# Four pairs of PSUM banks for the up products, and the last output slice finished by column halves

## The reference

```python
up = rms_norm(x, g_ffn_norm) @ w_up              # (512 + 32) x 1024 times 1024 x 5632
up_c, ffn_buf_new = causal_dwconv(up, ffn_buf, ffn_conv_w, ffn_conv_b)   # width 3
gate, val = jnp.split(up_c, 2, axis=-1)
x = x + (jax.nn.silu(gate) * val) @ w_down       # times 2816 x 1024
```

## Time and profile before

| | us |
|---|---|
| three runs, median (lowest to highest) | 945.11 (944.52 to 946.34) |
| the profiled execution, its own time | 945.21 |
| its span, first to last instruction | 943.3 |
| PE busy in it | 899.4 |
| up products, about | 527 to 799 |
| down products, about | 800 to 938 |

### The profile page before, as it was taken

How to read it: one execution, slowest core, us unless ns; L and a number is a source line. 1 busy time by engine, 2 the same in 40 slices (tenths; PEclk the granted TensorE clock), 3 DMA queues, 4 the chain that set the end, 5 groups by cost and what they waited for, 6 DMA issues and landing times.

```text
span 943.3 us, 18508 instructions
## 1 busy us (share of the span) xinstructions
PE 899.4 (95%) x6689; PEld 847.8 (90%) x6689; DVE 604.8 (64%) x1182; ACT 347.5 (37%) x619; POOL 238.3 (25%) x278
## 2 busy tenths in 40 slices
PE   5999999998799999998999999999999999999998
PEld 5899999987577887776799999999999999999998
DVE  4378634686789888897544488777778777322221
ACT  6331455364344444442423533333333332112111
POOL 4000233462333221331012233333333333201000
PEclk8999999999899999997999999999999999999999
DMA  8333323322000000010003232233332222233321
GB/s 256 79 84 76 97 78 82 77 73 46 15 7 10 14 14 14 20 27 1 1 23 90 67 110 78 81 88 89 89 89 82 78 85 84 84 97 104 98 70 36
DMA packets 114630, 63.55 MB, mean 67 GB/s; under 512 B 7836, under 2 KB 113054, under 8 KB 114588
## 3 DMA queue, kind: packets, MB, share of 16 engines
q1 hardware_dynamic: 112396, 59.17, 22.4%
q0 software_dynamic: 2192, 3.81, 1.8%
HBM read 59.85 MB, written 2.70 MB: 66 GB/s over the span
## 4 chain that ended last, share of the span: by engine, by line
PE 86%; DVE 6%; issue 4%; ACT 2%; POOL 1%; SPq 1%; DMA 0%; DVEq 0%; ACTq 0%; POOLq 0%
PE PS L1141 61%; PE PS L1354 4%; PE PS L1338 4%; PE PS L1319 3%; PE PS L1176 3%; PE PS L1265 2%; PE PS L1308 2%; PE PS L1214 2%; PE PS L1261 1%; PE PS L1362 1%; PE PS L1292 1%; PE PS L1283 1%; DVE small L1010 1%; DVE w_lo L773 0%; PE PS L1325 0%
## 5 line engine op out<-in xcount | busy, mean ns | idle before, releaser
L541 ACT ACTIVATE w_hi<-w_raw 128x1024 fp32r<-128x1024 f32 (+2 forms) x104 | 107.6, 1035 | 368.7 <-PE PS L1141 354.4
L773 DVE TENSOR_TENSOR w_lo<-w_raw,w_hi 128x1024 fp32r<-128x1024 f32 (+2 forms) x104 | 128.1, 1231 | 122.8 <-ACT w_hi L541 122.6
L1141 PE MATMUL PS<-x2h,w_hi 128*128 128x274 f32 x704 | 147.7, 291 | 1.1 <-DVE w_lo L773 1.1
L1141 PE MATMUL PS<-x2h,w_lo 128*128 128x274 f32 x704 | 146.9, 290 | 0.0
L1141 PE MATMUL PS<-x2l,w_hi 128*128 128x274 f32 x704 | 146.9, 290 | 0.0
L1141 PEld LDWEIGHTS PS<-x2h,w_hi 128*128 128x128 f32 x704 | 111.9, 189 | 1.4 <-issue 1.3
L1141 PEld LDWEIGHTS PS<-x2l,w_hi 128*128 128x128 f32 x704 | 112.0, 189 | 0.0
L1141 PEld LDWEIGHTS PS<-x2h,w_lo 128*128 128x128 f32 x704 | 111.4, 189 | 0.0
L1141 PE MATMUL PS<-xnh,w_hi 128*128 128x274 f32 x384 | 83.3, 299 | 4.4 <-DVE w_lo L773 2.3
L1141 PE MATMUL PS<-xnl,w_hi 128*128 128x274 f32 x384 | 81.7, 295 | 0.0
L1141 PE MATMUL PS<-xnh,w_lo 128*128 128x274 f32 x384 | 81.0, 293 | 0.0
(11 more groups left out here) (254 smaller groups left out, 1706.6 us busy)
## 6 DMA issues: line engine op xcount, KB each, us to landing
w_raw<-in_w_up_dram SPq DMA_DIRECT2D x44, 512.0 KB, 3.8
w_raw<-in_w_in_dram SPq DMA_DIRECT2D x24, 512.0 KB, 3.9
w_raw<-in_w_down_dram SPq DMA_DIRECT2D x16, 512.0 KB, 3.7
w_raw<-in_w_out_dram SPq DMA_DIRECT2D x8, 512.0 KB, 4.1
w_raw<-in_w_down_dram SPq DMA_DIRECT2D x8, 384.0 KB, 3.9
xnat<-in_x_prompt_dram SPq DMA_DIRECT2D x4, 512.0 KB, 5.0
w_raw<-in_w_in_dram SPq DMA_DIRECT2D x4, 416.0 KB, 4.7
wq<-in_w_q_b_dram SPq DMA_DIRECT2D x8, 192.0 KB, 2.5
```

Of the source, the lines that this page charges most:

```text
L541: nc.scalar.activation(hi[:, slot % 2, 0:n], raw[:, slot % 4, 0:n], ACT.Copy).then_inc(s_hi, 1)
L773: tt(lo[:, slot % 2, 0:n], raw[:, slot % 4, 0:n], hi[:, slot % 2, 0:n].bitcast(F32), ALU.subtract).then_inc(s_lo, 1)
L1141: last = mm(PS[:, 2 * rank + j, 0:HT], w[:, slot % 2, cols], x[:, k0 + k, j * HT:(j + 1) * HT], start=(k0 + k == 0 and first), stop=(k0 + ...
```

## The change

Two parts. **Up:** product r uses banks 2r and 2r+1 for r = 0 to 3 (`up_pair`), PE waits for the evacuation of the product four before it, and waits in addition on `s_ms` before the first use of banks 4 and 5 and on `s_stc` before that of banks 6 and 7. **Tail:** product 7 is written out as `last_product`. Its first two items run as before; the transposes of slice 6 are moved behind the first item; the 36 matmuls of the last item run as 18 for the left column half and then 18 for the right. DVE adds the residual by halves, PE transposes frames 0 to 255 and then frames 256 to 511 with the sample's (`last_y`, banks 6, 0 and 1), ACT copies the two parts, SP stores each part. The sample's rows are copied by DVE and stored by the POOL queue.

```diff
+        def up_pair(r):
+
+            return PS[:, 2 * r:2 * r + 2, 0:HT]
...
-            for m in range(KD - 2, KD):
-                sp.wait_ge(s_yn, 2 * m + 2)
-                sp.dma_start(y_p[:, :, m * P:(m + 1) * P], ynat[:, m % 2, 0:NT, :]).then_inc(s_ylast, 16)
-                sp.dma_start(o[1][0][:, m * P:(m + 1) * P], ynat[0:DEC, m % 2, NT, :]).then_inc(s_ylast, 16)
+            m = KD - 2
+            sp.wait_ge(s_yn, 2 * m + 2)
+            sp.dma_start(y_p[:, :, m * P:(m + 1) * P], ynat[:, m % 2, 0:NT, :]).then_inc(s_ylast, 16)
+            sp.dma_start(o[1][0][:, m * P:(m + 1) * P], ynat[0:DEC, m % 2, NT, :]).then_inc(s_ylast, 16)
+            m = KD - 1
+            for part in range(2):
+                sp.wait_ge(s_yn, 2 * m + 1 + part)
+                sp.dma_start(y_p[:, 2 * part:2 * part + 2, m * P:(m + 1) * P], ynat[:, m % 2, 2 * part:2 * part + 2, :]).then_inc(s_ylast, 16)
             sp.wait_ge(s_ylast, 16 * 4)
...
-            pool.wait_ge(s_out, 16 * 6)
+            m = KD - 1
+            pool.wait_ge(s_ysample, 1)
+            pool.dma_start(o[1][0][:, m * P:(m + 1) * P], ynat[0:DEC, m % 2, NT, :]).then_inc(s_out, 16)
+            pool.wait_ge(s_out, 16 * 7)
...
-            y_natural(KD - 1, (KD - 1) % 2)
+            last, s = KD - 1, (KD - 1) % 2
+            act.wait_ge(s_yout[s], 32 * (last // 2))
+            for part in range(2):
+                act.wait_ge(s_yt, last + 1 + part)
+                nc.scalar.activation(ynat[:, s, 2 * part:2 * part + 2, :], PS[:, (6, 0)[part], 0:2 * P].rearrange("p (a b) -> p a b", a=2), ACT.Copy).then_inc(s_yn, 1)
...
-                    tt(halves(u_r[:, LEAD:]), pair(r), halves(rsT[:, :]), ALU.mult).then_inc(s_free, 1)
+                    tt(halves(u_r[:, LEAD:]), up_pair(r), halves(rsT[:, :]), ALU.mult).then_inc(s_free, 1)
...
-                dve.wait_ge(s_used, I_DOWN + 3 * (m + 1))
                 if m >= 2:
                     dve.wait_ge(s_yt, m - 1)
+                if m == KD - 1:
+                    for j in range(2):
+                        dve.wait_ge(s_used, I_DOWN + 3 * (m + 1) + j)
+                        cols = slice(j * HT, (j + 1) * HT)
+                        tt(yT[:, m % 2, cols], PS[:, 2 * (m % 2) + j, 0:HT], xT[:, m, cols], ALU.add).then_inc(s_free, 1)
+                    break
+                dve.wait_ge(s_used, I_DOWN + 3 * (m + 1))
                 tt(halves(yT[:, m % 2, :]), pair(m), halves(xT[:, m, :]), ALU.add).then_inc(s_free, 1)
+
+            last, s = KD - 1, (KD - 1) % 2
+            dve.wait_ge(s_yt, last + 2)
+            dve.wait_ge(s_yout[s], 32 * (last // 2))
+            nc.vector.tensor_copy(ynat[0:DEC, s, NT, :], PS[0:DEC, 1, 0:P]).then_inc(s_ysample, 1)
...
             for r in range(4):
-                pe.wait_ge(s_free, G_UP + r - 1)
-                product(x2h, x2l, r % 2, [(I_UP + r, r, 0, KD)], (s_xl, KD) if r == 0 else None, x2_sums if r == 0 else None)
+                pe.wait_ge(s_free, G_UP + min(r - 1, 0))
+                if r == 2:
+                    pe.wait_ge(s_ms, 1)
+                if r == 3:
+                    pe.wait_ge(s_stc, 1)
+                product(x2h, x2l, r, [(I_UP + r, r, 0, KD)], (s_xl, KD) if r == 0 else None, x2_sums if r == 0 else None)
             with pe.Fori(1, NU // 4) as it:
-                products(it, G_UP, x2h, x2l)
+                for r in range(4):
+                    pe.wait_ge(s_free, it * 4 + (G_UP + r - 3))
+                    product(x2h, x2l, r, [(it * 4 + (I_UP + r), r, 0, KD)])
...
+            def last_product(m):
+
+                x_parts = ((hi, hh), (hi, hl), (lo, hh))
+                for j, q in ((None, 0), (None, 1), (0, 2), (1, 2)):
+                    k0, slot = KD * q, (3 * m + q) % 2
+                    pe.wait_ge(s_lo, I_DOWN + 3 * m + q + 1)
+                    for k in range(k0, min(k0 + KD, KF)):
+                        cols = slice((k - k0) * P, (k - k0 + 1) * P)
+                        for n, (w, x) in enumerate(x_parts):
+                            for jj in (0, 1) if j is None else (j,):
+                                last = mm(PS[:, 2 * (m % 2) + jj, 0:HT], w[:, slot, cols], x[:, k, jj * HT:(jj + 1) * HT],
+                                          start=(k == 0 and n == 0), stop=(k == KF - 1 and n == 2))
+                    last.then_inc(s_used, 1)
+                    if q == 0:
+                        y_transpose(m - 1)
+
+            def last_y(m):
+
+                s = m % 2
+                pe.wait_ge(s_yn, 2 * m - 2)
+                for part in range(2):
+                    pe.wait_ge(s_free, G_DOWN + m + 1 + part)
+                    for t, (c0, _, n) in list(enumerate(TOK))[2 * part:2 + 3 * part]:
+                        dst = PS[0:n, (6, 0)[part], t % 2 * P:(t % 2 + 1) * P] if t < NT else PS[0:n, 1, 0:P]
+                        last = nc.tensor.transpose(dst, yT[:, s, c0:c0 + n], ident[:, :])
+                    last.then_inc(s_yt, 1)
+
             for m in range(KD):
                 items = [(I_DOWN + 3 * m + q, 3 * m + q, KD * q, min(KD, KF - KD * q)) for q in range(3)]
-                pe.wait_ge(s_free, G_DOWN + m - 1)
+                pe.wait_ge(s_free, G_DOWN + (m - 3 if m < 2 else m - 1))
+                if m == KD - 1:
+                    last_product(m)
+                    last_y(m)
+                    break
...
-            y_transpose(KD - 1)
```

More of the change, by code:

```diff
@@ L272, in layer @@
         s_gc, s_sg, s_h2, s_hh, s_hl = sem("gate_conv"), sem("gate_silu"), sem("hidden"), sem("hidden_hi"), sem("hidden_lo")
-        s_yt, s_yn = sem("y_transposed"), sem("y_natural")
+        s_yt, s_yn, s_ysample = sem("y_transposed"), sem("y_natural"), sem("last_sample_natural")
         block = ctx.enter_context(nc.Block())
```

## The result

The changed kernel took 950.37 us (median of 6 runs, 948.85 to 951.0) against 944.82 us for the kernel before beside it: a ratio of 1.0057, interval 1.0043 to 1.0071. It is slower by 0.6%, and 4 us above the range that was given.

The account below looks back on a forecast made before the run. TensorE, busy 899.4 of 943.3 us, was taken to bound the kernel. Up 0; tail +0.55, -0.30, -0.22, -0.38 and the stores' landing came to about -0.4 us: median 944.7 us, range 943.5 to 946.1.

Parts of the forecast that it names:

- The up part: Up products through four pairs of banks: worth 0, since TensorE's only wait there names w_lo, not a bank.
- the gap: TensorE's wait before the third up product, 1.07 us, for w_lo; claimed to stay.
- The bound of 0.3 us for short pauses: Up products: most that pauses too short for the wait list could cost over 2148 matmuls, from the pitch difference.
- Steps 1 to 7 of the tail: Last product to SP's stores: transposes uncovered +0.55 us, half add -0.30, fewer transposes -0.22, shorter copy -0.38; landing at 942.17.
- Step 8: Sample's last rows: VectorE copies, POOL issues the store at 940.17, landing 2.2 us later at 942.37, the last landing.
- Rival 2: POOL's sample store lands last after 4.0 us: +1.3 us, 946.4 us; chance 0.09.
- rival 3: The 36 last-item matmuls into one bank don't overlap, pitch 0.29 us: +5.8 us, 950.5 us; chance 0.02.
- Step 9: End of span: 0.42 us after the last landing gives 942.79; POOL noticing up to 0.27 us later, half counted: 942.9.
- three signs of being wrong: Gap at 540 us closes, the 36 matmuls take over 4.7 us, or POOL's store takes more than 2.7 us.

Follow-up runs that it names:

- e3: Kernel before with only the up products' rotation through four pairs of banks; 945.54 us, ratio 0.9994.
- e7: Kernel before (two pairs of banks) with VectorE making the w_lo split before the evacuation in an up product; 945.25 us, ratio 1.0006.
- e8: Changed kernel with the sample's last store on SP, plus VectorE's w_lo split put before the evacuation (four pairs); 943.97 us, ratio 0.9989.
- e1: Changed kernel with the sample's last store issued by the SP queue behind its two parts instead of by POOL; 944.11 us, ratio 0.9986.
- e5: The changed kernel measured again, nothing altered; 949.35 us, ratio 1.0046 to the kernel before.
- e2: Kernel before with one more wait at the end of POOL's list, no transfer added or moved; 946.62 us, ratio 1.0014.
- e6: Changed kernel with POOL still issuing the sample's store but SP waiting for its landing; 947.39 us, ratio 1.0026.

## Why the prediction was wrong

**The up part** was right in all: no row had TensorE waiting for a bank, the gap named w_lo and stayed, and e3 measured no change. The bound of 0.3 us for short pauses wasn't needed: with four pairs the 2148 matmuls took 274.68 us (e3), with two 274.69. e7 and e8 confirm the reading of the gap from the other side.

**Steps 1 to 7 of the tail** were right in sign and nearly in size. From the mark to the last matmul the changed kernel took 0.56 us more (405.89 against 405.33), for the five transposes whose cover was gone. The 36 matmuls into one bank cost nothing. In the changed kernel they start from 935.44 us on:

```profile
935.57 0.29 PE L1483 MATMUL PS<-hl,w_hi 128*128 128x274 f32 x1
...
939.79 0.29 PE L1483 MATMUL PS<-hl,w_hi 128*128 128x274 f32 x1
```

Between these two are 33 steps, 4.22 us, 127.9 ns each. The right add took 0.44, three transposes 0.55, the copy 0.38 us (0.36 expected). The stores landed sooner than assumed, 128 KB in 1.8 us and not 2.2. With the sample on SP (e1) all this comes to -0.8 us from the mark, where the forecast said -0.4 and -0.8 at best.

**Step 8** had POOL's issue right (941.90 against 940.17 + 1.7 for the later start) and its landing too long (1.9 us, not 2.2). Rival 2, which feared the landing, did not come true. Nor did rival 3, although its time of 950.5 us is nearly the measured 950.37: that is chance, since its mechanism, a longer pitch in one bank, was absent.

**Step 9 is the one that failed.** "With the 0.42 us of the end: 942.79. POOL may notice the landing up to 0.27 us later than SP did (0.30 against 0.03)." The 0.42 us was read from an execution in which SP was the last to finish, and was given to one in which POOL is. In its place came 0.2 us until POOL's list was over, its DRAIN of 4.72 us, and 0.3 us to the end of the span: 5.2 us in place of 0.4 to 0.7. In step 8 the text says of POOL's queue that "all that is queued behind is its own wait for landings"; behind that wait stood the DRAIN, which no line of the code names. The row was there in the trace of the kernel before, at L112, 4637 ns long and hidden under product 7: its cover, 12.9 us between its end and the span's, was the thing to ask for when POOL's list was made to last to the end. With it, and with nothing but the rows of the kernel before, the sum reads 942.37 + 0.42 + 4.64 = 947.4 us, 4.2 us over the span of 943.3, and a forecast of 949.3 us. None of the three signs of being wrong that the prediction named appeared: the gap stayed, the 36 matmuls took 4.6 us and POOL's store 1.9. Signs can only be named for terms that the sum has, and the DRAIN was not one of them.

The medians gave 4.6 and 5.5 us where the profiles give 4.0. The second interval (3.1 to 5.7) holds 4.0, the first (4.1 to 6.7) just misses it. That the rest is scatter of the start is what e5 and the spread of the marks suggest; it is not shown run by run.

**The range.** It was said to join the forecast's bounds with the scatter of the runs. These give 944.3 - 0.6 = 943.7 and 945.3 + 1.2 = 946.5, not 943.5 to 946.1. The measured time lies outside either.

## What to carry to other kernels

Before work is moved to the end of an engine's list, look at how that engine's list closes: the closing row of each queue is in the trace, and a long one may be hidden now. A late store costs less on a queue that is in use to the end anyway (here SP) than on an engine that would have been finished. A wait that names one producer may hide a second one right behind it, so a change that frees the second is worth nothing until the first is moved. A measured time that matches a rival's number doesn't show the rival: look for its mechanism in the rows.

## What the runs showed of the hardware

- POOL's closing DRAIN grew with the transfers that POOL had issued in the whole execution: 3.168, 3.658, 4.637 and 4.719 us for 38, 44, 56 and 57 of them, 0.082 us each, also where POOL's last one had been issued 17 us before (e2). Those of SP and of the compute engines were 0.007 to 0.81 us. In e6, where the last of 57 transfers had not landed when it began, it took 5.03 us.
- The first half of an execution scatters by 3.4 us between kernels that are alike there (the mark at 530.95 to 534.33 us), and by 1.4 us between two executions of the changed kernel (534.33 and 532.97). The granted clock from 15 to 60 us, 0.87 to 0.96, goes with it; what sets that clock stays open. In the 29 runs of the kernel before beside e5 the time goes with the mean granted clock too: 943.6 us on average at 0.985 (4 runs), 944.3 at 0.984 (8), 945.4 at 0.982 (11), 946.1 at 0.980 (6).
- 18 matmuls running into one bank of PSUM kept the pitch of matmuls that alternate between two, 127.9 against 127.7 to 127.9 ns at 274 columns.
